# Two row gathers become one over a joined expert table, with pairs handled singly and the top-k made two heads ahead

## The chip, the cores and the metric

The kernel runs on one core of one Trainium2 chip. Times are device microseconds (us) of one execution of the whole program; the time before is a median of three runs. The profile is one further execution, recorded by the hardware profiler. Engines are called as in the profile: PE (TensorE, with PEld for its weight loads), DVE (VectorE), ACT (ScalarE), POOL (GpSimd) and SP (SyncE).

## The reference

Two transformer blocks run one after the other on 512 tokens of width 1024, in float32. The first (neighbourhood attention, a convolution branch, a mixture of experts) and the attention of the second are not touched by the change. What is touched is the last layer, `peer_layer`, for 512 tokens, 8 heads and 16 experts per head:

```python
query = (ht @ w_query).reshape(t, PEER_HEADS, 2, PEER_HALF)
sub_scores = jnp.einsum('thpd,hpkd->thpk', query, sub_keys)          # 2 x 128 scores per head
half_vals, half_idx = lax.top_k(sub_scores, PEER_TOPK)               # 16 of each half
cand = half_vals[:, :, 0, :, None] + half_vals[:, :, 1, None, :]     # 256 sums
top_vals, top_pos = lax.top_k(cand.reshape(...), PEER_TOPK)          # 16 of them
experts = i1 * PEER_N_KEYS + i2                                      # one of 16384 per pick
gates = jax.nn.softmax(top_vals, axis=-1)
...
u = expert_down[eb]                                                  # a row of 1024 per pick
act = jax.nn.gelu(jnp.einsum('td,thkd->thk', xb, u)) * gb
vv = expert_up[eb]                                                   # another row of 1024
return jnp.einsum('thk,thkd->td', act, vv)
```

So each token reads, for each of 8 heads, 16 rows of `expert_down` and the 16 rows of `expert_up` with the same numbers.

## The kernel before

Tokens lie on the 128 partitions, so there are four token tiles t, and a "head" n runs from 0 to 31 (8 heads for each of 4 tiles; `TT = 4`, `H = 8`, `K16 = 16`). All work is ordered by hand: each engine has its own program, and semaphores join them.

**One head.** ACT copies the head's queries to `qh` (`queries`, L1252). PE multiplies them with the sub keys into bank 0 (`peer_scores`, L2371). DVE does the top-k: L1742 to L1746 find 16 of 128 twice, L1759 makes 256 sums, L1742 to L1746 find 16 of these, L1766 prepares the softmax, L1768 to L1777 work out the expert numbers, and L1780 writes them to `ids`. ACT does the softmax's exponential (`gate_exp`, L1256). POOL gathers rows of 4 KB for each of 128 partitions: L837 from the down table and L847 from the up table, 16 of each per head, one indirect DMA for each pick. DVE makes the dot products (L1794), four picks to a group; ACT applies Gelu to four (L1260); DVE multiplies by the gates (`gated`, L1800); ACT makes a diagonal matrix for each pick (L1267); PE multiplies this with the up row, in two halves of 512 columns, and sums over all heads in PSUM (`up_sums`, L2380).

**Buffers.** There are 8 buffers for down rows (two sets of four) and 8 for up rows while tile 0 is worked on, 16 after that. A set of four comes free at once: the down set after its fourth dot product (`down_free`), the up set after its last product on PE (`up_free`).

**Order.** In `gathers`, POOL first waits for the head's `ids`, then issues group by group (down 0, down 1, up 0, down 2, up 1, down 3, up 2, up 3). On DVE the whole top-k of head n+1 stands between dot groups 1 and 2 of head n:

```python
dot(n, t, 0)
dot(n, t, 1)
gated(n, b, 0)
if more:
    topk_halves(nxt)
    topk_pairs(nxt, 1 - b)
    gates(nxt, 1 - b)
dot(n, t, 2)
```

**Tile 0.** Its 8 heads run together with the attention of the tiles 1 to 3 of the same block. That attention is cut into steps (`attend`), and `PLAN` spreads the steps 6 to 66 over 8 heads of 8 parts each, by weights; the two last are projections of the queries for head 0 and 1 of the later tiles (`query_b`, L1875). The other six `query_b` run on PE during the heads of tile 1; SP loads 1 MB of weights for each.

**End of a tile.** `last_norm` on DVE and ACT adds the tile's sums to the residual, normalises and lets SP write it out. PE closes a tile's sums with L2404.

Of the kernel before, what the change touches and what calls it, by code (L numbers as in the profile page):

```python
# [25 lines left out]
P = 128  # L26
T = 512
# [28 lines left out]
G4 = 4  # L56
DOWN_SETS = 2
GROUPS = K16 // G4
UP_FIRST, UP_SETS = 2, GROUPS

# [17 lines left out]
def build(nc, A, out):  # L78
    with ExitStack() as ctx:
# [196 lines left out]
        gate_p = [small(704 + K16 * i, K16) for i in range(2)]  # L276
# [10 lines left out]
        up += [hold_b[:, 3 * D:4 * D], arena_q[:, 3 * D:4 * D], arena_h[:, 0:D], arena_h[:, D:2 * D]]  # L287
        up += [hold_a[:, 2 * D:3 * D], hold_a[:, 3 * D:4 * D], arena_v[:, 6144:6144 + D], arena_v[:, 7168:7168 + D]]

        def up_set(n, g):  # L290

            per = 16 * G4
            if n[1] < H:
                return g % UP_FIRST, (per * GROUPS // UP_FIRST, per * (g // UP_FIRST + 1))
            at = (g + UP_FIRST) % GROUPS
            before = per * GROUPS // UP_FIRST * H if at < UP_FIRST else 0
            return at, (per, per + before - per * H)


        def up_used(n, g):  # L300

            return at_head(n, GROUPS, UP_FIRST + g + 1)
# [11 lines left out]
        x_in = sem("x_in")  # L314
        modb_in = sem("modb_in")
        cw_in = sem("cw_in")
        modb2_in = sem("modb2_in")
        modb3_in = sem("modb3_in")
        rpb_in = sem("rpb_in")
# [5 lines left out]
        mcol2_in = sem("mcol2_in")  # L325
        mod_out_rest = sem("mod_out_rest")
        mcol_in = sem("mcol_in")
        xres_in = sem("xres_in")
# [62 lines left out]
        fn_in = sem("fn_in")  # L391
# [47 lines left out]
        down_free = sem("down_free")  # L439
        up_free = sem("up_free")  # L440
# [7 lines left out]
        last_rows_in = sem("last_rows_in")  # L448
        down_in = [sem(f"down_in{i}") for i in range(DOWN_SETS)]
        up_in = [sem(f"up_in{i}") for i in range(UP_SETS)]  # L450
# [102 lines left out]
        EXP_LN = "natural_log_exp_and_others"  # L553

# [19 lines left out]
        AHEAD = 2  # L574
        STEPS = ST_QUERY + AHEAD
# [4 lines left out]
        PLAN = [[[s for s in range(LEAD, STEPS) if int(sum(weight[LEAD:s]) / sum(weight[LEAD:]) * (H * PARTS - 4)) == h * PARTS + p]  # L580
# [5 lines left out]

        def at_head(n, per, extra):

            i, off = n
            return per * off + extra if i is None else i * (2 * per) + (per * off + extra)  # L590
# [15 lines left out]
        def _(sp):  # L606
# [110 lines left out]
            for dst, src in ((gt2_2, mod2_d[0, 5 * D:6 * D]), (gfin, A["g_final_2"])):  # L717
                sp.dma_start(dst, src.partition_broadcast(P)).then_inc(last_rows_in, 16)
# [5 lines left out]
            sp.wait_ge(skew_out, 16)  # L724
# [4 lines left out]
        def _(pool):  # L729
# [21 lines left out]
            for r, dst in ((0, mcol), (1, mcol_c)):  # L751
# [5 lines left out]
                           A["rpb"].rearrange("h r c -> (h r) c")).then_inc(rpb_in, 16)  # L757
            pool.wait_ge(rpb_in, 16)
# [17 lines left out]
            pool.wait_ge(skew_out, 16)  # L776
# [23 lines left out]
            pool.dma_start(mcol_2[:, :, :], mod2_d[0, 0:2 * D].rearrange("(k p c) -> p k c", k=2, c=DC)).then_inc(mcol2_in, 16)  # L800
# [9 lines left out]
            pool.dma_start(fn_b, A["final_norm"].partition_broadcast(P)).then_inc(fn_in, 16)  # L810
# [19 lines left out]
            pool.sem_inc(down_free, DOWN_SETS)  # L830

            def down_rows(n, b, g):
                pool.wait_ge(down_free, at_head(n, GROUPS, g + 1))
                pool.sem_inc(mark, 1)
                for k in range(G4):
                    r = G4 * g + k
                    pool.indirect_dma_start(down[r % (G4 * DOWN_SETS)], None, A["expert_down_2"],  # L837
                                            bass.IndirectOffsetOnAxis(ap=ids[b][:, r:r + 1], axis=0)).then_inc(down_in[g % DOWN_SETS], 16)

            def up_rows(n, b, g):  # L840
                at, _ = up_set(n, g)

                pool.wait_ge(up_free, up_used(n, g - (UP_FIRST if n[1] < H else UP_SETS)))
                pool.sem_inc(mark, 1)
                for k in range(G4):
                    r = G4 * g + k
                    pool.indirect_dma_start(up[G4 * at + k], None, A["expert_up_2"],  # L847
                                            bass.IndirectOffsetOnAxis(ap=ids[b][:, r:r + 1], axis=0)).then_inc(up_in[at], 16)

            def ids_ready(n):  # L850
                pool.wait_ge(ids_done, at_head(n, 1, 1))
                pool.sem_inc(mark, 1)

            def gathers(n, b):
                ids_ready(n)
                down_rows(n, b, 0)
                for g in range(1, GROUPS):
                    down_rows(n, b, g)
                    up_rows(n, b, g - 1)
                up_rows(n, b, GROUPS - 1)  # L860


            ids_ready((None, 0))
            down_rows((None, 0), 0, 0)
            down_rows((None, 0), 0, 1)
            for h in range(H):
                n, nxt, b = (None, h), (None, h + 1), h % 2
                for g in range(2):
                    down_rows(n, b, 2 + g)
                    up_rows(n, b, g)  # L870
                if h + 1 < H:
                    ids_ready(nxt)
                for g in range(2):
                    if h + 1 < H:
                        down_rows(nxt, 1 - b, g)
                    up_rows(n, b, 2 + g)

            pool.wait_ge(qh_done, H + 1)
            pool.wait_ge(q_done, 4 + 2 * AHEAD)
            for t in range(1, TT):  # L880
                with pool.Fori(0, H // 2) as i:
                    for b in range(2):
                        gathers((i, t * H + b), b)

        @block.scalar
        def _(act):
# [48 lines left out]
            for m in range(18):  # L935
# [12 lines left out]
                if m == 9:  # L948

                    for i, b in enumerate((A["b_mod"][4 * T:8 * T], A["b_mod"][8 * T:12 * T], A["b_ada_2"][0:4 * T])):  # L950
                        act.dma_start(mod_bias[i][0:P:32, :], b.rearrange("(j n) -> j n", n=T)).then_inc(modb2_in, 16)
# [291 lines left out]
            def queries(n):  # L1243
                i, off = n
                if off > 0:
                    act.wait_ge(sc_pe, at_head(n, 1, 0))
                    act.sem_inc(mark, 1)
                if i is None:
                    src = qT2_a[:, off, :] if off < H else qT2_b[:, off - H, :]
                else:  # L1250
                    src = qT2_b[:, bass.ds(i * 2 + (off - H), 1), :].rearrange("p a b -> p (a b)")
                act.activation(qh.rearrange("p a b -> p (a b)"), src, ACT.Copy).then_inc(qh_done, 1)  # L1252
# [17 lines left out]
            def peer_head(n, more, query=None):  # L1270
# [3 lines left out]
                if more:  # L1274
                    queries(nxt)
# [1193 lines left out]
```

## Time and profile before

| | |
|---|---|
| median of 3 runs | 3359.75 us (3359.63 to 3369.18) |
| span of the profiled execution | 3579.5 us |
| PE busy | 2668.3 us, 75% of the span |
| DVE busy | 1426.3 us, 40% |
| POOL busy | 1154.3 us, 32% |
| ACT busy | 709.3 us, 20% |
| DMA, mean over the span | 259 GB/s |
| mean granted TensorE clock | 0.856 |

The profiled execution is 219.75 us longer than the median, 6.5%. Its own time is therefore its span, first to last instruction; nothing of it lies outside. Times from the profile are compared with this span, and carried over to the median by the ratio 3359.75 / 3579.5 = 0.939. Busy shares are means over stages with different limits, so they are read stage by stage below.

### The profile page before, as it was taken

How to read it: one execution, taken by the hardware profiler on the slowest of the kernel's cores; microseconds unless marked ns; L12 is line 12 of the kernel's file. 1: busy time of each engine (PE TensorE's matmuls, PEld its weight loads, DVE VectorE, ACT ScalarE, POOL GpSimd, SP SyncE). 2: the span in 40 equal slices, each digit the busy share in tenths (PEclk: the TensorE clock that was granted, in tenths of full speed). 3: DMA queues.
4: the chain of work that ended last, by engine and by line, in shares of the span. 5: the costliest groups of instructions: out<-in, count | busy, mean ns of one | idle time of the engine just before them, and what ended most of it. 6: DMA issues, size and time to landing. Idle time of an engine off the chain costs nothing.

```text
span 3579.5 us, 28389 instructions
## 1 busy us (share of the span) xinstructions
PE 2668.3 (75%) x8698; PEld 1311.5 (37%) x8698; DVE 1426.3 (40%) x3490; ACT 709.3 (20%) x1634; POOL 1154.3 (32%) x1113
## 2 busy tenths in 40 slices
PE   2998999767777766988779987767675565475566
PEld 1445544423333323556555434333332222232232
DVE  1376400410000003014655465544555555555554
ACT  2015400110000003122342322111112121121111
POOL 1001100000000000001434454656565666666665
PEclk8999999778889987988888899888887787787788
DMA  7328618369999964212666677888887888888887
GB/s 248 128 71 292 210 51 241 143 263 384 377 382 389 397 259 164 94 47 89 239 233 245 248 276 258 315 319 298 307 321 295 335 313 312 313 318 307 320 297 277
DMA packets 281055, 927.91 MB, mean 259 GB/s; under 512 B 27001, under 2 KB 67000, under 8 KB 264062
## 3 DMA queue, kind: packets, MB, share of 16 engines
q0 software_dynamic: 154432, 558.29, 42.6%
q1 hardware_dynamic: 116736, 359.68, 27.4%
q10 hardware_dynamic: 9790, 8.73, 0.7%
q8 instruction: 51, 0.84, 0.1%
q14 instruction: 46, 0.38, 0.0%
HBM read 891.42 MB, written 35.18 MB: 259 GB/s over the span
## 4 chain that ended last, share of the span: by engine, by line
PE 43%; DVE 13%; issue 10%; DVEq 4%; ACT 3%; DMA 2%; POOL 2%; ACTq 1%; another core or an unknown queue 1%; POOLq 0%; SPq 0%
PE bank L2380 18%; PE bank L2081 8%; PE bank L1875 6%; DVE ring L1794 4%; PE bank L2094 3%; DVEq L1737 3%; PE bank L1881 2%; DVEq L1739 1%; POOL ring L837 1%; DMA ring<-in_expert_down,ids 1%; ACTq L1049 1%; ACT arena_h L1267 1%; DVE arena_w L1776 1%; PE bank L2204 1%
## 5 line engine op out<-in xcount | busy, mean ns | idle before, releaser
L2380 PE MATMUL bank<-ring,arena_h 128*128 128x512 f32 x1568 | 771.2, 648 | 508.2 <-ACT arena_h L1267 484.0
L837 POOL DMA_INDIRECT ring<-in_expert_down,ids x512 | 559.0, 1092 | 929.2 <-DVE ids L1780 474.3
L2380 PEld LDWEIGHTS bank<-ring,arena_h 128*128 128x128 f32 x1568 | 321.6, 210 | 916.8 <-ACT arena_h L1267 503.6
L1794 DVE CUSTOM_DVE_ANT_0 ring<-ring 128x1024 f32<-128x1024 f32 x384 | 447.8, 1223 | 204.9 <-DMA ring<-in_expert_down,ids 162.1
L847 POOL DMA_INDIRECT ring<-in_expert_up,ids x392 | 392.3, 1001 | 141.6 <-issue 118.2
L1875 PE MATMUL bank<-arena_h,ring 128*128 128x512 f32 (+1 forms) x1024 | 372.1, 524 | 17.6 <-DMA ring<-in_w_in 15.4
L2081 PE MATMUL bank<-ring,arena_h 128*64 128x512 f32 x1056 | 289.7, 710 | 65.0 <-ACT arena_h L1040 61.9
L1875 PEld LDWEIGHTS bank<-arena_h,ring 128*128 128x128 f32 x1024 | 178.5, 196 | 200.4 <-issue 197.4
L1576 DVE TENSOR_TENSOR arena_q<-arena_q,bank 128x256 f32<-128x256 f32 x32 | 13.5, 421 | 525.2 <-ACT arena_q L1043 525.2
L824 POOL DMA_INDIRECT arena_v<-ys_d,slot_i x8 | 8.0, 1001 | 601.6 <-SPq L675 591.4
L2081 PEld LDWEIGHTS bank<-ring,arena_h 128*64 128x64 f32 x1056 | 98.8, 161 | 231.4 <-issue 196.3
L1794 DVE CUSTOM_DVE_ANT_0 ring<-ring,arena_w 128x1024 f32<-128x1024 f32 x128 | 149.3, 1222 | 56.0 <-DMA ring<-in_expert_down,ids 44.3
L1267 ACT ACTIVATE arena_h<-ident,arena_w 128x128 f32<-128x128 f32 x512 | 159.0, 388 | 6.6 <-DVE arena_w L1800 6.0
L1260 ACT ACTIVATE arena_w<-arena_w 128x4 f32<-128x4 f32 x128 | 24.3, 202 | 626.2 <-DVE arena_w L1794 605.4
L2094 PE MATMUL bank<-ring,arena_q 128*64 128x512 f32 x528 | 120.6, 597 | 21.1 <-DVE arena_q L1579 20.5
L1881 PE MATMUL bank<-ring,arena_h 128*128 128x512 f32 x224 | 101.2, 612 | 1.0 <-ACT arena_h L1203 0.8
L1417 DVE SCALAR_TENSOR_TENSOR arena_x<-arena_x,convc 128x512 f32<-128x512 f32 x120 | 90.2, 752 | 4.3
L1256 ACT ACTIVATE arena_w<-arena_w 128x16 f32<-128x16 f32 x32 | 6.9, 216 | 401.2 <-DVEq L1771 148.7
L2380 PE MATMUL bank<-arena_v,arena_h 128*128 128x512 f32 x192 | 86.3, 592 | 0.0
L2380 PE MATMUL bank<-arena_h 128*128 128x512 f32 x192 | 86.3, 592 | 0.0
L1875 PE MATMUL bank<-arena_q,ring 128*128 128x384 f32 x224 | 80.0, 514 | 8.1 <-issue 8.1
L768 POOL DMA_DIRECT2D mod_d<-arena_v x20 | 10.0, 500 | 232.3 <-DVE arena_v L1402 230.2
(453 smaller groups left out, 3113.3 us busy)
## 6 DMA issues: line engine op xcount, KB each, us to landing
ring<-in_w_exp_gate SPq DMA_DIRECT2D x33, 2048.0 KB, 7.9
ring<-in_w_exp_up SPq DMA_DIRECT2D x33, 2048.0 KB, 12.7
ring<-in_w_exp_down SPq DMA_DIRECT2D x33, 2048.0 KB, 14.3
ring<-in_w_in SPq DMA_DIRECT2D x15, 2048.0 KB, 23.3
ring<-in_w_mod SPq DMA_DIRECT2D x12, 2048.0 KB, 9.8
ring<-in_w_ada SPq DMA_DIRECT2D x12, 2048.0 KB, 16.9
xs_d<-zeros SPq DMA_DIRECT2D x1, 12032.0 KB, 69.5
arena_h<-xs_d SPq DMA_DIRECT2D x33, 256.0 KB, 13.7
```

The lines of the kernel that those rows point to most:

```text
L837: pool.indirect_dma_start(down[r % (G4 * DOWN_SETS)], None, A["expert_down_2"], bass.IndirectOffsetOnAxis(ap=ids[b][:, r:r + 1], axis=0)). ...
L847: pool.indirect_dma_start(up[G4 * at + k], None, A["expert_up_2"], bass.IndirectOffsetOnAxis(ap=ids[b][:, r:r + 1], axis=0)).then_inc(up_i ...
L1049: act.dma_start(ys_d[bass.ds(e * CAP, CAP), 512 * half:512 * half + 512], yblk[b][CAP * half:CAP * half + CAP, :]).then_inc(y_dma[b], 16)
L1267: d = act.activation(diag[:, r, :], ident[:, :], ACT.Copy, scale=coef[:, r:r + 1])
L1417: link(dve.scalar_tensor_tensor(out=conv[:, cc, :], in0=u_pad[:, cc, k:k + T], scalar=convc[:, cc, k:k + 1], in1=conv[:, cc, :], op0=ALU.m ...
L1737: dve.wait_ge(topk_step, at_head(n, TOPK_STEPS, k))
L1794: d = dve.tensor_tensor_reduce(buf, buf, h2r_2[t], 1.0, 0.0, ALU.mult, ALU.add, dots[:, r:r + 1])
L1875: mm = pe.matmul(dst, w[:, c, at], rhs[:, c, :], start=(c == 0), stop=(c == chunks - 1))
L1881: mm = pe.matmul(dst, xT[:, c, t * P:(t + 1) * P], w[:, c, at], start=(c == 0), stop=(c == chunks - 1))
L2081: mm = pe.matmul(bank[2 + b][at, :].rearrange("p (g f) -> p g f", g=2), xbT[b][:, c, :], gu[:, :, c, 256 * half:256 * half + 256], start=( ...
L2094: mm = pe.matmul(bank[6 + b][CAP * j:CAP * j + CAP, :], hidT[b][:, k, CAP * half:CAP * half + CAP], slab(n)[:, half, k, 512 * j:512 * j + ...
L2380: mm = pe.matmul(bank[4 + 2 * (t % 2) + j][:, :], diag[:, G4 * g + k, :], up[G4 * at + k][:, 512 * j:512 * j + 512], start=False, stop=False)
```

## The change

The host joins `expert_down` and `expert_up` side by side into one table with rows of 2048 numbers. One indirect DMA then brings both rows of a pick, 8 KB for each partition, into one "pair" buffer: the dot product reads its first half, PE its second.

- Buffers: 8 pairs for tile 0, 11 after it. Each pair has its own semaphore for landing, and comes free by itself when PE has done its product.
- Top-k: for head n+2 during head n, cut into six pieces, which stand in parts 2 to 7 between pairs of dot products. Top-k of head 1 runs ahead of head 0.
- The multiplication by the gates goes from DVE (one for four picks) to ACT (one for each pick). Gelu takes four picks at once for tile 0 and two after that.
- Attention steps are spread over 6 heads (47 parts) in place of 8 (60 parts). `query_b` 2 to 7 follow the heads 6 to 11, whole.
- `last_norm` of tile t-1 runs after head 6 of the tile t in place of at its end (tile 3's stays at the end). The loops over heads are written out, and some semaphores are merged.

```diff
+PAIRS_0, PAIRS = 8, 11
...
-        down = [ring[:, 2 + r // 4, D * (r % 4):D * (r % 4) + D] for r in range(G4 * DOWN_SETS)]
-        up = [ring[:, 4 + r // 4, D * (r % 4):D * (r % 4) + D] for r in range(G4 * UP_FIRST)]
...
+        pair = [ring[:, 2 + k // 2, 2 * D * (k % 2):2 * D * (k % 2) + 2 * D] for k in range(PAIRS_0)]
+        pair += [hold_a[:, 2 * D:4 * D], arena_v[:, 6144:6144 + 2 * D], arena_h[:, 0:2 * D]]
...
+        LAST_AT = 6
...
+        FRONT = 6
...
-        PLAN = [[[s for s in range(LEAD, STEPS) if int(sum(weight[LEAD:s]) / sum(weight[LEAD:]) * (H * PARTS - 4)) == h * PARTS + p]
+        PLAN = [[[s for s in range(LEAD, STEPS) if int(sum(weight[LEAD:s]) / sum(weight[LEAD:]) * (FRONT * PARTS - 1)) == h * PARTS + p]
...
+            for n in range(TT * H):
+                pool.wait_ge(ids_done, n + 1)
+                for r in range(K16):
+                    m = n * K16 + r
...
+                    if pair_before(m) >= 0:
+                        pool.wait_ge(pair_free, pair_before(m) + 1)
+                    pool.sem_inc(mark, 1)
+                    pool.indirect_dma_start(pair[pair_of(m)], None, A["expert_pair_2"],
+                                            bass.IndirectOffsetOnAxis(ap=ids[n % 2][:, r:r + 1], axis=0)).then_inc(pair_in[pair_of(m)], 16)
...
+            def coefs(n, r0, count):
+
+                m = n * K16 + r0
+                act.wait_ge(dots_done, m + count)
+                act.activation(gel[:, r0:r0 + count], dots[:, r0:r0 + count], ACT.Gelu).then_inc(gelu_done, 1)
+                act.wait_ge(gelu_done, m // count + 1 + (0 if n < H else FIRST // 4 - FIRST // 2))
+                for r in range(r0, r0 + count):
+                    act.activation(coef[:, r:r + 1], gel[:, r:r + 1], ACT.Copy, scale=gate_p[n % 3][:, r:r + 1]).then_inc(coef_done, 1)
+                act.wait_ge(coef_done, m + count)
+                if n > 0:
+                    act.wait_ge(pair_free, m + count - K16)
+                for r in range(r0, r0 + count):
+                    act.activation(diag[:, r, :], ident[:, :], ACT.Copy, scale=coef[:, r:r + 1]).then_inc(diag_done, 1)
...
+            def topk_part(n, part):
+
+                if part in (2, 3):
+                    topk_half(n, part - 2)
                 elif part == 4:
+                    topk_sums(n)
                 elif part == 5:
+                    topk_pairs(n)
                 elif part == 6:
+                    topk_halves_of(n, 0)
                 elif part == 7:
+                    topk_halves_of(n, 1)
+                    topk_ids(n)
+
+            def dot(n, r):
+                m = n * K16 + r
+                dve.wait_ge(pair_in[pair_of(m)], 16 * pair_turn(m))
+                buf = pair[pair_of(m)][:, 0:D]
+                dve.tensor_tensor_reduce(buf, buf, h2r_2[n // H], 1.0, 0.0, ALU.mult, ALU.add, dots[:, r:r + 1]).then_inc(dots_done, 1)
+
+            def peer_part(n, part):
+                dot(n, 2 * part)
+                dot(n, 2 * part + 1)
+                if n + 2 < TT * H:
+                    topk_part(n + 2, part)
...
+            def up_sums(n, r):
+                m = n * K16 + r
+                pe.wait_ge(diag_done, m + 1)
+                for j in range(2):
+                    mm = pe.matmul(bank[4 + 2 * (n // H % 2) + j][:, :], diag[:, r, :], pair[pair_of(m)][:, D + 512 * j:D + 512 * j + 512],
+                                   start=False, stop=False)
+                mm.then_inc(pair_free, 1)
...
+    inputs["expert_pair_2"] = np.concatenate([inputs["expert_down_2"], inputs["expert_up_2"]], axis=-1)
```

## Rows read from the trace of the kernel before

**Rows 1.** The page: engines, granted clock and DMA by slice of the span.
```profile
span 3579.5 us, 28389 instructions
PE 2668.3 (75%) x8698; PEld 1311.5 (37%) x8698; DVE 1426.3 (40%) x3490; ACT 709.3 (20%) x1634; POOL 1154.3 (32%) x1113
...
PEclk8999999778889987988888899888887787787788
DMA  7328618369999964212666677888887888888887
```

**Rows 2.** Four stages: busy us of each engine, granted clock, DMA share, GB/s.
```profile
1000.00:1300.00 300.00, 238.64 (x1011) 94.64 (x1009) 14.38 (x34) 26.84 (x51) 0.00 (x0) 0.91 1.00 390
1670.00:2244.00 574.00, 491.25 (x1733) 284.77 (x1732) 333.33 (x819) 187.70 (x417) 262.95 (x251) 0.87 0.68 244
2244.00:2642.00 398.00, 281.62 (x667) 131.93 (x665) 195.44 (x512) 66.23 (x182) 245.74 (x229) 0.85 0.86 320
2642.00:3552.00 910.00, 532.01 (x1182) 233.73 (x1183) 510.31 (x1295) 172.06 (x447) 586.53 (x542) 0.79 0.84 313
```

**Rows 3.** Timeline: expert numbers of heads 0, 15, 31 written; PE's L2404, first and last.
```profile
1670.01 0.17 DVE L1780 CAST ids<-arena_w 128x16 int32<-128x16 f32 x1
...
2642.54 0.17 DVE L1780 CAST ids<-arena_w 128x16 int32<-128x16 f32 x1
3497.23 0.17 DVE L1780 CAST ids<-arena_w 128x16 int32<-128x16 f32 x1
...
L2404 PE MATMUL bank<-zeros x32: 592/592/595, 1671.3 to 3568.7; 128*128 128x512 f32 x32
```

**Rows 4.** Timeline of POOL over one head: start, us, instruction, [idle before].
```profile
3023.29 1.21 POOL L837 DMA_INDIRECT ring<-in_expert_down,ids  x1 [9.47 <-DVE arena_w L1794]
3024.81 1.98 POOL L837 DMA_INDIRECT ring<-in_expert_down,ids  x1 [0.30 <-issue]
3027.09 0.94 POOL L837 DMA_INDIRECT ring<-in_expert_down,ids  x1 [0.30 <-issue]
3028.34 0.94 POOL L837 DMA_INDIRECT ring<-in_expert_down,ids  x1 [0.30 <-issue]
...
3066.88 0.93 POOL L847 DMA_INDIRECT ring<-in_expert_up,ids  x1 [0.31 <-issue]
3076.49 1.21 POOL L837 DMA_INDIRECT ring<-in_expert_down,ids  x1 [8.68 <-DVE arena_w L1794]
```

**Rows 5.** Top-k of head 0 on DVE, with POOL idle: first and last but one.
```profile
1657.30 0.30 DVE L1742 MAX8 arena_w<-bank 128x8 f32<-128x128 f32 x1 [20.61 <-PE bank L2371]
...
1669.80 0.17 DVE L1777 SCALAR_TENSOR_TENSOR arena_w<-arena_w 128x16 f32<-128x16 f32 x1
```

**Rows 6.** Dot products and top-k of one later head on DVE, with POOL issuing.
```profile
3034.12 1.23 DVE L1794 CUSTOM_DVE_ANT_0 ring<-ring 128x1024 f32<-128x1024 f32 x1 [6.55 <-DMA ring<-in_expert_down,ids]
3035.27 0.08 DVE L1794 DVE_READ_ACCUMULATOR2_ANT arena_w<- 128x1 f32 x1
3035.27 1.22 DVE L1794 CUSTOM_DVE_ANT_0 ring<-ring 128x1024 f32<-128x1024 f32 x1
...
3046.87 0.30 DVE L1742 MAX8 arena_w<-bank 128x8 f32<-128x128 f32 x1 [2.49 <-PE bank L2371]
...
3059.01 0.43 DVE L1773 TENSOR_TENSOR arena_w<-iota,arena_w 128x256 f32<-128x256 f32 x1 [2.46 <-issue]
...
3068.78 0.17 DVE L1780 CAST ids<-arena_w 128x16 int32<-128x16 f32 x1 [1.93 <-issue]
```

**Rows 7.** Short stretches within one head; columns as in Rows 2.
```profile
3020.00:3025.00 5.00, 1.02 (x2) 0.51 (x3) 5.00 (x12) 1.41 (x5) 1.40 (x2) 0.50 0.00 0
3025.00:3030.00 5.00, 5.00 (x11) 2.28 (x10) 2.38 (x6) 2.81 (x10) 4.08 (x4) 0.81 0.81 243
...
3055.00:3060.00 5.00, 0.00 (x0) 0.00 (x0) 1.60 (x7) 1.59 (x3) 3.78 (x5) 0.76 1.03 419
3060.00:3065.00 5.00, 0.00 (x0) 0.00 (x0) 1.70 (x4) 0.00 (x0) 3.78 (x5) 0.50 1.03 410
```

**Rows 8.** Timeline of PE: products of up rows and a `query_b`.
```profile
2213.12 7.03 PE L2380 MATMUL bank<-ring,arena_h 128*128 128x512 f32 x16
2219.98 10.48 PE L1875 MATMUL bank<-arena_q,arena_v 128*128 128x384 f32 x32
```

**Rows 9.** PE's L2380 alone in the tile 0 stage: busy, clock, DMA share, GB/s.
```profile
1670.00:2244.00 574.00, 228.90 (x475) 0.87 0.68 244
```

**Rows 10.** Groups of instructions on ACT.
```profile
L1267 ACT ACTIVATE arena_h<-ident,arena_w 128x128 f32<-128x128 f32 x512 | 159.0, 388 | 6.6 <-DVE arena_w L1800 6.0 <-issue 0.4
L1260 ACT ACT_TABLE_LOAD x45 | 57.7, 1283 | 0.8
L1260 ACT ACTIVATE arena_w<-arena_w 128x4 f32<-128x4 f32 x128 | 24.3, 202 | 626.2 <-DVE arena_w L1794 605.4 <-issue 20.6
```

More of the change, by code:

```diff
@@ L275, in build @@
         gsub, gex = small(672, K16), small(688, K16)
-        gate_p = [small(704 + K16 * i, K16) for i in range(2)]
+        gate_p = [small(704 + K16 * i, K16) for i in range(2)] + [sb("gate_c", [P, K16])[:, :]]
         dots, gel, coef = small(736, K16), small(752, K16), small(768, K16)
@@ L447, in build @@
         rows2_in = sem("rows2_in")
-        last_rows_in = sem("last_rows_in")
-        down_in = [sem(f"down_in{i}") for i in range(DOWN_SETS)]
-        up_in = [sem(f"up_in{i}") for i in range(UP_SETS)]
+        pair_in = [sem(f"pair_in{i}") for i in range(PAIRS)]
         yg_in = [sem(f"yg_in{t}") for t in range(TT)]
@@ L854, in gathers @@
[L854 to L876, printed above, removed]
@@ new lines, in peer_head @@
+            def peer_head(n):
+                for p in range(PARTS):
+                    if p == 0 and n + 2 < TT * H:
+                        queries(n + 2)
+                    if p == 6 and n + 2 < TT * H:
+                        gate_exp(n + 2)
+                    coefs(n, 2 * p, 2)
+            def peer_part(n, part):
+                if part == 0:
+                    queries(n + 2)
+                if part == 6:
+                    gate_exp(n + 2)
+                if part % 2 == 1:
+                    coefs(n, 2 * part - 2, 4)
+                    if any(s < ST_FOX for parts in PLAN[n:] for steps in parts for s in steps):
+                        act.preload_act_table_set(EXP_LN)
@@ L1789, in dot @@
-            def dot(n, t, g):
-                dve.wait_ge(down_in[g % DOWN_SETS], at_head(n, 16 * G4 * (GROUPS // DOWN_SETS), 16 * G4 * (g // DOWN_SETS + 1)))
-                for k in range(G4):
-                    r = G4 * g + k
-                    buf = down[r % (G4 * DOWN_SETS)]
-                    d = dve.tensor_tensor_reduce(buf, buf, h2r_2[t], 1.0, 0.0, ALU.mult, ALU.add, dots[:, r:r + 1])
-                d.then_inc(down_free, 1)
-            def gated(n, b, g):
-                at = slice(G4 * g, G4 * g + G4)
-                dve.wait_ge(gelu_done, at_head(n, GROUPS, g + 1))
-                dve.tensor_tensor(coef[:, at], gel[:, at], gate_p[b][:, at], ALU.mult).then_inc(coef_done, 1)
@@ L1856, in _ @@
                         attend(s)
[L1857 to L1867 removed]
+            for n in range(H, TT * H):
+                for part in range(PARTS):
+                    peer_part(n, part)
+                if n % H == LAST_AT:
+                    if n // H == 1:
+                        dve.wait_ge(rows2_in, 16 * 10)
+                    last_norm(n // H - 1)
             last_norm(TT - 1)
@@ L2401, in edge, with peer_part @@
+            def peer_part(n, part):
+                if part == 1:
+                    peer_scores(n + 2)
+                if part % 2 == 0 and n + part > 0:
+                    for r in range(4):
+                        up_sums(n if part else n - 1, (2 * part - 4 + r) % K16)
             def edge(t, first):
```

366 lines of the change are left out of this document (116 added, 250 removed).

## The prediction

> **What bounds the kernel now.** I read the page's slices first, then the stages, then one head on POOL, DVE and the DMA engines. On the page [rows 1] no engine but PE is over 40% busy, while in the last two fifths the DMA digit stands at 7 or 8. The stages [rows 2] say where this begins. Tile 0 with attention beside it (1670 to 2244 us) has PE busy for 491 of 574 us and DMA at 0.68. Afterwards PE is busy 58% of the time (532 of 910 us), DVE 56%, POOL 64% and the DMA engines 0.84 at 313 GB/s. So in the later stage no resource is full, and the question is what leaves them idle in turn.
>
> Rows 3 give the pace: from head 15's numbers to head 31's there are 16 heads in 854.7 us, 53.4 us each. One head on POOL [rows 4] shows what fills it. From 3023.29 to 3067.81 POOL issues 32 gathers without a pause; the common one takes 0.94 us and 0.30 us of issue, 1.24 us, and some take 1.98. That is 44.5 us. Then POOL stands for 8.68 us, until DVE has made dot products again. DVE has not made any because the top-k stands between its dot groups: with POOL idle the top-k takes 12.9 us (1657.30 to 1670.18) [rows 3, 5], with POOL issuing it takes 22 us (3046.87 to 3068.95), with waits such as 2.46 us in front of an operation [rows 6]. So the loop is POOL's 32 issues, plus a hole made by the top-k: 44.5 + 8.7 = 53.2 us. In the hole the DMA engines run dry (0.00 and 0 GB/s), while just before they run at 410 to 419 GB/s [rows 7]. PE, which gets its pairs late, stands too, and its granted clock is at 0.50 (1.2 GHz) in the slice before its restart and 0.81 in the slice after.
>
> **The change, part by part.** I cost the stretch from the first head's numbers (1670.2) to the last product (3568.7): 1898.5 us [rows 3]. The 1670 us ahead are left as they are but for merged semaphores, which I cost at nothing, as the same transfers are waited for. The 10 us behind (the last norm) stay.
>
> *Later heads, 12 to 31.* The bytes stay: 16 picks x 128 rows x 8 KB = 16.78 MB a head.
> - POOL: 16 issues in place of 32. If a pair costs what a row does, 16 x 1.24 = 19.8 us, and if each meets a dot product and takes 1.98 + 0.30, 36.5 us. No trace row has a gather of 8 KB rows. Below, I take the same cost, since the number of rows to be addressed is the same; above, twice 0.94. Either way POOL can be under the DMA time.
> - DVE: 16 dots at a pitch of 1.15 us [rows 6] are 18.4 us; a wait ahead of each may add 0.1, so 20. The top-k is 12.9 us with POOL idle and 22 with POOL always issuing. POOL would issue for 1.24 of each 2.7 us, so about half of the 9 us extra: 17.5. `gated` is gone. Sum 37.5 us, under the DMA time but near it.
> - ACT: per two picks one Gelu (0.20), two coefficients (about 0.20 each, as the small Gelu) and two diagonals (0.39 each) [rows 10], 1.4 us, and with the hand-overs some 2 us; 8 x 2 = 16, and two table loads of 1.28: 19 us. The coefficients that moved here (3.2 us a head) are hidden behind a DMA pace of 5.4 us for two picks.
> - PE: 64 records a head at 7.03 / 16 = 0.44 us [rows 8] is 28 us at full clock.
> - DMA: the longest saturated stretch of this trace moved 390 GB/s at share 1.00 for 300 us [rows 2]; the gathers reach 410 to 419 for some 15 us [rows 7]. 16.78 MB take 43.0 us at 390, 40.4 at 415, 45.0 at 373 (313 / 0.84, what a full share would give at this stage's efficiency). I take 43.0, because it is the rate that was held longest.
> - Buffers: a pair lives from issue to PE's product. From the end of the fourth issue (3029.28) to the dot of that group (3034.12) are 4.8 us. Add 1.2 for the issue, up to 3.5 for a piece of top-k in front, 2.4 for two dots, 2 for ACT, 3.5 for two products on PE: 17.4 us. Eleven buffers at 2.7 us cover 29.6 us, so the gathers stay ahead and POOL no longer waits on DVE's top-k. The numbers for head n+1 are there before head n begins, so this wait goes altogether.
> So 20 x 43.0 = 860 us. The stall moves from POOL to the DMA queue.
>
> The Trainium skill, "DMA: Bandwidth & Descriptors", section Specifications, gives a limit of about 358 GB/s of HBM for a core. By that a head would take 46.9 us and this change would give 26 x 3.9 = 101 us less of what I count. The trace has 390 and 419 GB/s, so it disagrees, and the sum goes by its rows.
>
> *Heads 6 to 11.* Each has a `query_b` behind it on PE, 32 records, 10.5 us [rows 8]: 28 + 10.5 is 38.5 us, still under DMA. SP's 1 MB of weights adds 1.05 / 0.39 = 2.7 us of DMA: 45.7. Heads 6 and 7 have 8 buffers and four picks to a Gelu: life of a pair near 24 us over 8 buffers is 3.0 us a pick, 48 us. So 2 x 48 + 4 x 45.7 = 279 us.
>
> *Heads 0 to 5, with the attention.* In 1670 to 2244, PE was busy 491.25 us, of which L2380 had 228.9 [rows 9]; the rest, 262 us, is attention and projections and must now fit in six heads. With six heads of products, 228.9 x 6 / 8 = 172, PE has 434 us. It stood for 83 us over 8 heads, 10.3 a head. Some of that was waiting for down rows behind late numbers, which goes; against this ACT swaps tables four times a head where it did twice, 2 x 2 x 1.28 = 5 us, and each step follows a longer chain. I keep 7.6 a head, 46 us. The early top-k of head 1 (12.9 us) stands where nothing of head 0 can run: 10 us. Sum 490 us. Bounds: 434 (no idle) to 584 (the old 574 us untouched, plus 10).
>
> *Total.* 490 + 279 + 860 = 1629 us for 1898.5: 270 us less, 3579.5 - 270 = 3309.5 us in the profile's own time. The median of the runs is shorter by 6.1%, so times 0.939: 3106 us. I say 3105.
>
> **The rivals.** All are counted in the median's time.
> - *DVE becomes the bound.* POOL's issues and DVE's operations hold each other up [rows 6]: with POOL issuing, the top-k takes 9 us more. If all of that stays and dots wait too, DVE needs 20 + 22 + 6 = 48 us a head. Heads 6 to 31: 1248 for 1139, +102: 3208 us. For it speaks that 37.5 is near 43; against it that POOL is silent half the time.
> - The Trainium skill, "SBUF — State Buffer", section SBUF: two separate sides, says that DVE and GpSimd share a port pair under an exclusive lock that is held for a whole instruction. The row's 2.46 us before L1773 agrees; by it alone half as many issues lock half as long.
> - *The front does not shrink.* If chains across engines, not PE, set tile 0, the steps take what they took: 584 us for 490, +88: 3193 us. For it: PE's 83 us idle. Against: PE busy 86%.
> - *DMA is slower than 390 GB/s.* At 373 the 26 heads take 2 us more each, +49: 3155 us.
> - *An 8 KB gather costs POOL double.* 1.88 + 0.30, and 1.04 more where a dot is met (1.98 - 0.94) [rows 4]: 3.22 x 16 = 51.5 us a head; 24 heads x 8.5 x 0.939, +192: 3300 us.
> - *The recorder slows what the change removes.* The profile is 219.75 us above the median. If all of this lay in POOL's issuing in the 32 heads, a head before takes 46 us unprofiled, and the change gives 270 - 220 = 50 us: 3310 us. Nothing in the trace tells this apart.
> - *Slower: PE stays at 1.2 GHz.* PE would work in bursts of 3.5 us with 1.9 us between them. If the clock stayed at 0.50 (1.2 GHz), the records take twice 0.44: 56 us a head and 77 with a `query_b`, 20 x 56 + 6 x 77 = 1582 for 1139: 3520 us. It decides once PE's own time for a head passes the 53.4 us of before, which needs nearly all of the head at 0.50. For it: PE idles in every head, as it does ahead of the 0.50 in rows 7. Against it: at 0.50 PE would have no idle time left, and in rows 7 the clock is 0.81 as soon as PE is busy through a slice.
> - *Nothing changes*, some loop of the same length taking over: 3360.
>
> **How the numbers follow.** Chances: forecast 0.42 (its own range 3060 to 3160), DVE bound 0.14, front 0.09, slower DMA 0.09, double POOL cost 0.05, recorder 0.09, clock 0.08, nothing 0.04. Faster is all but the last two: 0.88; within 0.3% (about 10 us, what a measurement here can tell from no change) 0.04; slower 0.08. The range begins at 3030: with 40.4 us a head (-63) and a front of 470 (-19) it would be 3024. Upwards it goes to 3310, to the two cases of 3300 and 3310 us, since without them 0.26 would be left out; with them 0.12 is, the two last. It also takes in two of the milder rivals together (3208 and +88).
>
> **What would show it.** Right: from some 2200 us on, the DMA share stays at 1.0 and 390 GB/s or more with no slice near 0; heads 12 to 30 come each 43 us, by the writing of the expert numbers; POOL waits mostly for PE's releases; the granted clock is above 0.9; the sixth head ends some 490 us after the first numbers. Wrong: DVE over 95% busy (DVE bound); gathers of near 1.9 us (double cost); PE busy throughout with the clock at 0.5 (clock); heads at 43 us but a median less than 150 us below the old one (recorder); the heads 0 to 5 over 560 us (front).

## The result: 3269 us for 3361 us, a third of the forecast gain

The changed kernel takes 3268.78 us (median of 4 runs, 3263.08 to 3270.47), the kernel before 3360.53 us. The ratio is 0.9703 with a 95% interval of 0.9677 to 0.9729, so it is 92 us faster. I had forecast 3105 us, 255 us faster; the direction is right and the size is not. The changed kernel's own profile spans 3261.3 us, 8 us from its median.

The page of the changed kernel, to be held against [rows 1]:

```profile
span 3261.3 us, 27350 instructions
...
PE 2663.6 (82%) x8698; PEld 1292.5 (40%) x8698; DVE 1425.1 (44%) x3362; ACT 872.7 (27%) x2245; POOL 661.9 (20%) x601
...
PEclk8999999968888989699789877999999999999998
DMA  7417814728999999512136745689999999999996
GB/s 248 164 52 241 300 61 143 244 95 321 386 377 380 393 387 384 199 65 67 38 128 226 290 163 224 243 317 369 418 417 421 421 421 421 421 398 421 421 421 278
```

POOL's busy time fell from 1154 to 662 us, the DMA digit stays at 9 in the last quarter but for the last slice, and the rate there is 421 GB/s in most slices. That is what the prediction described. The next view says what it was worth. These are the stages of the changed kernel by token tile (columns as in [rows 2]); each ends where PE closes the tile's sums:

```profile
1670.00:2267.00 597.00, 530.65 (x1833) 303.79 (x1831) 346.27 (x835) 247.19 (x587) 137.33 (x135) 0.87 0.66 253
2267.00:2599.00 332.00, 284.27 (x681) 126.86 (x680) 237.56 (x583) 118.07 (x364) 152.64 (x131) 0.97 1.01 419
2599.00:2924.00 325.00, 248.91 (x552) 101.58 (x551) 240.42 (x586) 117.39 (x365) 163.16 (x129) 0.97 1.00 415
2924.00:3249.00 325.00, 247.38 (x548) 100.23 (x547) 218.71 (x505) 110.71 (x354) 152.21 (x119) 0.97 0.96 400
```

A later head takes 325 / 8 = 40.6 us (40.7 by the writing of the expert numbers), with a DMA share of 1.00 and a granted clock of 0.97. The stretch I had costed at 1629 us measures 1579 us. So the changed kernel is, if anything, a little better than I had worked out, and the gain is still a third. The error has to be in what it was compared with, and the first experiment asks that.

### The profile page after: what moved, and what is told of

It is laid out like the page before. It is cut to its first block, busy times and chain, and to the rows that moved or that the text cites. A ratio compares the mean times of both kernels' runs of the same rounds, so it can differ in the third digit from the quotient of the medians.

```text
span 3261.3 us, 27350 instructions
## 1 busy us (share of the span) xinstructions
PE 2663.6 (82%) x8698; PEld 1292.5 (40%) x8698; DVE 1425.1 (44%) x3362; ACT 872.7 (27%) x2245; POOL 661.9 (20%) x601
## 4 chain that ended last, share of the span: by engine, by line
PE 38%; DMA 20%; DVE 7%; ACT 6%; issue 4%; ACTq 1%; POOL 1%; DVEq 0%; POOLq 0%; SPq 0%
DMA ring<-in_expert_pair,ids 15%; PE bank L2290 9%; PE bank L1995 9%; PE bank L1789 6%; PE bank L2008 4%; PE bank L1795 3%; DMA arena_v<-in_expert_pair,ids 3%; DVE ring L1744 2%; DMA arena_h<-in_expert_pair,ids 1%; ACTq L1002 1%; PE bank L2118 1%; PE bank L2117 1%; ACT arena_h L1219 1%; POOL ring L835 1%; ACT arena_w L1214 1%
## 5 line engine op out<-in xcount | busy, mean ns | idle before, releaser
L2290 PE MATMUL bank<-ring,arena_h 128*128 128x512 f32 x1772 | 840.9, 624 | 183.0 <-ACT arena_h L1219 182.9
L835 POOL DMA_INDIRECT ring<-in_expert_pair,ids x443 | 519.5, 1173 | 1161.3 <-PE bank L2290 633.0
L2290 PEld LDWEIGHTS bank<-ring,arena_h 128*128 128x128 f32 x1772 | 340.0, 198 | 652.6 <-issue 370.2
L1744 DVE CUSTOM_DVE_ANT_0 ring<-ring 128x1024 f32<-128x1024 f32 x315 | 383.8, 1225 | 177.3 <-DMA ring<-in_expert_pair,ids 158.0
L1789 PE MATMUL bank<-arena_h,ring 128*128 128x512 f32 (+1 forms) x1024 | 373.0, 525 | 15.6 <-DMA ring<-in_w_in 13.5
L1211 ACT ACTIVATE arena_w<-arena_w 128x2 f32<-128x2 f32 (+1 forms) x224 | 45.4, 203 | 627.1 <-DVE arena_w L1744 626.8
L1219 ACT ACTIVATE arena_h<-ident,arena_w 128x128 f32<-128x128 f32 x512 | 174.1, 393 | 7.3
L1795 PE MATMUL bank<-ring,arena_h 128*128 128x512 f32 x224 | 100.9, 610 | 1.0 <-ACT arena_h L1156 0.8
L2290 PE MATMUL bank<-arena_v,arena_h 128*128 128x512 f32 x140 | 70.3, 626 | 21.5 <-ACT arena_h L1219 21.5
L1214 ACT ACTIVATE arena_w<-arena_w 128x1 f32<-128x1 f32 x352 | 81.8, 285 | 5.0
L1795 PE MATMUL bank<-ring,arena_q 128*128 128x512 f32 x176 | 78.9, 609 | 3.6 <-DVE arena_q L1406 3.6
L2290 PE MATMUL bank<-arena_h 128*128 128x512 f32 x136 | 66.8, 614 | 17.5 <-ACT arena_h L1219 17.5
```

The source lines that it names most:

```text
L835: pool.indirect_dma_start(pair[pair_of(m)], None, A["expert_pair_2"], bass.IndirectOffsetOnAxis(ap=ids[n % 2][:, r:r + 1], axis=0)).then_i ...
L1211: act.activation(gel[:, r0:r0 + count], dots[:, r0:r0 + count], ACT.Gelu).then_inc(gelu_done, 1)
L1214: act.activation(coef[:, r:r + 1], gel[:, r:r + 1], ACT.Copy, scale=gate_p[n % 3][:, r:r + 1]).then_inc(coef_done, 1)
L1219: act.activation(diag[:, r, :], ident[:, :], ACT.Copy, scale=coef[:, r:r + 1]).then_inc(diag_done, 1)
L1744: dve.tensor_tensor_reduce(buf, buf, h2r_2[n // H], 1.0, 0.0, ALU.mult, ALU.add, dots[:, r:r + 1]).then_inc(dots_done, 1)
L1789: mm = pe.matmul(dst, w[:, c, at], rhs[:, c, :], start=(c == 0), stop=(c == chunks - 1))
```

## The experiments

### The kernel before, recorded once more

The file is unchanged.

> The kernel before, unchanged, once more. Theory A (the profiled execution on which the prediction stood was itself about 220 us slower than the median runs, in the gather stage, and the changed kernel's own profile is not): this execution has a span within 10 us of 3360, its stretch up to 1670 us is as before, and heads 15 to 31 come every 46 us or so in place of 53.4. Rival B (recording always adds 220 us to the kernel before): the span is again near 3580 and only the unrecorded runs are near 3360. Ratio to the kernel before 1.00 either way.

Measured: ratio 1.0003 (0.9977 to 1.003), and a profile that spans 3374.5 us, not 3579.5. Theory A holds, though the span is 14.5 us above 3360 where I had said within 10, and the first numbers come at 1678 us, 8 us later. The same four tiles in this second recording:

```profile
1676.00:2254.00 578.00, 513.76 (x1789) 293.93 (x1789) 340.77 (x833) 191.72 (x428) 282.80 (x268) 0.87 0.70 257
2254.00:2637.00 383.00, 312.74 (x745) 146.31 (x744) 243.15 (x622) 80.63 (x218) 282.15 (x260) 0.90 0.98 372
2637.00:2996.00 359.00, 255.69 (x553) 111.77 (x552) 237.95 (x616) 83.75 (x211) 281.83 (x254) 0.86 0.98 370
2996.00:3363.00 367.00, 265.03 (x551) 114.54 (x550) 225.78 (x573) 75.05 (x202) 279.26 (x245) 0.85 0.95 356
```

A head of tiles 2 and 3 takes 45.4 us (726 / 16), not the 53.4 us of [rows 3]. The hole that the prediction made its first term is not there. Its POOL timeline shows a stretch with dot products, then the top-k (2908.9 to 2921.8), then dot products again:

```profile
2901.45 1.98 POOL L847 DMA_INDIRECT arena_h<-in_expert_up,ids  x1 [0.30 <-issue]
2903.74 0.93 POOL L847 DMA_INDIRECT arena_h<-in_expert_up,ids  x1 [0.30 <-issue]
2904.98 1.27 POOL L837 DMA_INDIRECT ring<-in_expert_down,ids  x1 [0.30 <-issue]
2906.56 1.98 POOL L837 DMA_INDIRECT ring<-in_expert_down,ids  x1 [0.31 <-issue]
2908.84 0.94 POOL L837 DMA_INDIRECT ring<-in_expert_down,ids  x1 [0.30 <-issue]
...
2917.54 0.94 POOL L837 DMA_INDIRECT ring<-in_expert_down,ids  x1 [0.31 <-issue]
...
2922.79 1.59 POOL L847 DMA_INDIRECT ring<-in_expert_up,ids  x1 [0.31 <-issue]
2924.69 1.98 POOL L847 DMA_INDIRECT ring<-in_expert_up,ids  x1 [0.30 <-issue]
```

POOL never waits for anyone; it only issues. And the top-k takes 13 us with POOL issuing beside it, as it does with POOL idle [rows 5], against 22 us in [rows 6]. From 2650 to 3050 us the 281 gathers take 1.123 us in the mean, and with 0.30 us of issue 32 of them are 45.5 us: the pace of a head. Among the 281, 41 take 1.7 us or more and 18 between 1.1 and 1.7; most of the rest are at 0.94.

The long issues are those that meet a dot product. These are the dot products during which the issues at 2904.98 and 2922.79 began, and a like pair of rows of the changed kernel, with 8 KB rows:

```profile
2904.21 1.23 DVE L1794 CUSTOM_DVE_ANT_0 ring<-ring 128x1024 f32<-128x1024 f32 x1 [0.43 <-DMA ring<-in_expert_down,ids]
2922.35 1.23 DVE L1794 CUSTOM_DVE_ANT_0 ring<-ring 128x1024 f32<-128x1024 f32 x1 [0.16 <-DVE arena_w L1786]
```
```profile
2800.39 1.23 DVE L1744 CUSTOM_DVE_ANT_0 ring<-ring 128x1024 f32<-128x1024 f32 x1 [0.43 <-DMA ring<-in_expert_pair,ids]
2800.67 1.75 POOL L835 DMA_INDIRECT ring<-in_expert_pair,ids  x1 [1.98 <-PE bank L2290]
```

The issues begin 0.77, 0.44 and 0.28 us after their dot product and take 1.27, 1.59 and 1.75 us: each ends 2.03 to 2.04 us after the dot product began. From 2650 to 3050 us this is so for every issue that begins 0.06 to 1.08 us after a dot product, 24 of 24 here and 75 of 75 in the changed kernel. So the issue stands until some 1.09 us of the dot product are over and then takes its own 0.94. One that begins within 0.05 us of the start mostly takes 1.98 and sometimes 0.94.

That leaves two readings. Either POOL's issuing is the bound, with its long issues, or the DMA engines are (their share is 0.98) and the long issues are a symptom of that.

### Two gathers for each pair

```diff
-                    pool.indirect_dma_start(pair[pair_of(m)], None, A["expert_pair_2"],
+                    for j, table in enumerate(("expert_down_2", "expert_up_2")):
+                        pool.indirect_dma_start(pair[pair_of(m)][:, j * D:(j + 1) * D], None, A[table],
```

> The changed kernel, but each pair is brought by two gathers of 4 KB rows from the two separate tables into the two halves of the pair buffer; all else stays. Theory A (the gain is that the gathers run ahead without a hole and the DMA engines stay full; the joined table only saves issues): POOL has 32 issues of 1.24 us a head, 39.7 us and up to 50 where dot products hold them up, so POOL, not DMA, sets the heads 15 to 31: 45 to 50 us in place of 40.8, total 3350 to 3400. Rival B (POOL's issues still hide under the DMA time): 41 to 43 us a head, total 3270 to 3310.

Measured: 3358.69 us, ratio 0.9985 (0.996 to 1.001). A head takes 44.5 and 45.4 us in tiles 2 and 3 (356.0 and 363.4 us). All the rest of the change (pairs handled singly, the top-k two heads ahead in pieces, gates on ACT) brings nothing in sum by itself; joining the gathers on top of it brings the whole gain. The sum hides two parts: against the second recording of the kernel before, tile 0 is 27 us longer here, tile 1 35 us shorter (two of its six `query_b`, 21 us of PE, now lie in tile 0) and tiles 2 and 3 3 us shorter each. Joining then takes 5, 17, 30 and 39 us off the four tiles. Joining the gathers without the rest was not tried. And 45 us a head fits both readings still, POOL's issuing and full DMA engines.

### Half of the bytes, with the same issues

```diff
+                        w = D if n < H else D // 2
+                        at = j * D + (w * (pair_turn(m) % 2) if n >= H else 0)
+                        pool.indirect_dma_start(pair[pair_of(m)][:, at:at + w], None,
+                                                A[table] if n < H else A[table].rearrange("e (a b) -> (e a) b", b=w),
```

> As the kernel with two gathers a pair, but from head 8 on each gather brings only 512 of the 1024 columns of a row (2 KB a partition), and the other half of the buffer keeps older rows; dot products and products on PE stay as long. So 32 issues a head as before, with half of the bytes. Theory A (with 4 KB rows POOL's issuing sets the pace: 32 x 1.24 us plus some 5.5 long ones x 1.04, 45.4 us a head): tiles 2 and 3 stay near 356 and 363 us, total 3340 to 3370, and the DMA share falls to some 0.55. Rival B (the DMA engines are full at 370 to 375 GB/s with 4 KB rows, their share being 0.98 to 0.99): the pace falls to the next limit, 38 to 41 us a head, total near 3230 to 3270.

Measured: 3415.66 us, ratio 1.0106 (1.0066 to 1.0146). With half of the bytes no head is faster; in tiles 2 and 3 they take 47.7 and 47.0 us, for 44.5 and 45.4. That is above the range of theory A (3340 to 3370 us) and far from rival B. The windows 2650 to 3050 us, first the two gathers of 4 KB rows, then of 2 KB:

```profile
2650.00:3050.00 400.00, 291.76 (x616) 118.23 (x617) 270.30 (x658) 131.77 (x410) 312.77 (x287) 0.94 0.99 378
```
```profile
2650.00:3050.00 400.00, 282.16 (x578) 113.36 (x577) 253.58 (x621) 121.72 (x380) 318.43 (x268) 0.92 0.62 177
```

The kernel before, in its second recording, has in the same window:

```profile
2650.00:3050.00 400.00, 283.17 (x606) 123.87 (x607) 264.88 (x676) 92.78 (x237) 314.59 (x281) 0.85 0.98 369
```

So the DMA engines were not the bound at 378 GB/s with two gathers a pair, although their share read 0.99. POOL is busy 313 to 318 of 400 us in all three, which with 0.30 us for each issue leaves it no idle time. The 2 KB kernel even has more long issues (56 of 268, for 29 of 287), and (1.189 + 0.30) us x 32 = 47.6 us is again its pace. That is why it is slower and not only no faster; why more of its issues meet a dot product was not looked into.

### Short dot products

The dot products take 256 of the 1024 columns and leave the others out; bytes and issues stay. The edit was made in three kernels: with two gathers a pair, for the kernel before, and for the changed kernel.

```diff
-                dve.tensor_tensor_reduce(buf, buf, h2r_2[n // H], 1.0, ...
+                buf = pair[pair_of(m)][:, 0:D // 4]
+                dve.tensor_tensor_reduce(buf, buf, h2r_2[n // H][:, 0:D // 4], 1.0, ...
```

> As the kernel with two gathers a pair, but the dot products read and write only 256 of the 1024 columns (some 0.4 us in place of 1.22). Bytes and issues stay. Theory A (POOL sets the pace and its long issues of 1.98 us are those that meet a dot product): the long issues nearly go, 39.7 to 41 us a head, total 3359 - 24 x 4.5 = about 3250, at 410 GB/s. Rival B (DMA full at 375 GB/s with 4 KB rows, long issues being a full ring): 45 us a head as before, total 3340 to 3360.

> The kernel before, but the dot products read and write only 256 of the 1024 columns, as in the short-dot kernel with two gathers a pair. Theory A (in the kernel before, too, POOL's 32 issues and those of them that a dot product holds up set the pace, 32 x 1.24 + 5.5 x 1.04 = 45.4 us a head): 40 to 42 us a head, total 3366 - 24 x 4 to 5 = 3245 to 3275, ratio 0.965 to 0.973. Rival B (in the kernel before the top-k or DVE's dots are on the path as the prediction said): the gain comes from DVE, 24 x 16 x 0.8 = 307 us less, ratio 0.91.

> The changed kernel, but the dot products read and write only 256 of the 1024 columns. Theory A (its heads 12 to 31 wait for the DMA engines at 421 GB/s, and POOL has time to spare): the later tiles stay within 2 us of 325, total 3250 to 3270 with a little less in tile 0. Rival B (POOL or DVE is close under the DMA time and takes part): total under 3240.

Measured: two gathers a pair 3278.57 us, ratio 0.9699 (0.9661 to 0.9738); the kernel before 3248.05 us, 0.9636 (0.9615 to 0.9658); the changed kernel 3248.38 us, 0.9651 (0.9623 to 0.9679). The groups on POOL from 2650 to 3050 us (instructions, busy us, mean ns, idle before and its releasers), first of the kernel before, second recording, then of the same with short dots:

```profile
L837 POOL DMA_INDIRECT ring<-in_expert_down,ids x140 | 145.1, 1036 | 42.7 <-issue 42.1 <-PE bank L2380 0.6
L847 POOL DMA_INDIRECT ring<-in_expert_up,ids x98 | 118.5, 1209 | 29.9 <-issue 29.0 <-DVE ids L1780 0.9
```
```profile
L837 POOL DMA_INDIRECT ring<-in_expert_down,ids x154 | 146.4, 951 | 57.2 <-issue 43.9 <-DVE arena_w L1794 13.3
L847 POOL DMA_INDIRECT ring<-in_expert_up,ids x106 | 101.9, 961 | 32.3 <-issue 29.3 <-DVE ids L1780 2.7 <-DVE arena_w L1794 0.3
```

Of 310 issues none takes 1.7 us; the head takes 41.4 us in tiles 2 and 3, and the rate is 409 GB/s. With two gathers a pair the head falls to 41.8 and 41.6 us, a little above the 39.7 to 41 expected, also at 409 GB/s. Nothing on the DMA side was changed. So the issues held up by dot products are what held the kernel before. The rival for the kernel before, DVE itself on the path, wanted a ratio of 0.91 and is out.

With the long issues gone, the kernel before and the changed kernel take the same time within their spread, 3248.05 and 3248.38 us. That equality is a sum of unequal parts: the tiles are 552, 350, 331 and 331 us in the one, 581, 330, 325 and 324 in the other. The later tiles of the changed kernel stay at 325.1 and 324.4 us with short dots: there POOL had time to spare. With full dot products it already waits, mostly until PE frees a pair:

```profile
L835 POOL DMA_INDIRECT ring<-in_expert_pair,ids x131 | 167.5, 1278 | 155.7 <-PE bank L2290 131.3 <-issue 24.4
```

The two next experiments tell whether the DMA engines or the number of buffers set that wait. The changed kernel's 20 us come from tiles 0 and 1, which were 596 and 332 us and are 581 and 330; I had expected 0 to 19.

### What would be next under the DMA time

One gather of 4 KB a pair in place of 8 (half of the bytes; PE multiplies what the buffer held before):

```diff
-                    pool.indirect_dma_start(pair[pair_of(m)], None, A["expert_pair_2"],
+                    pool.indirect_dma_start(pair[pair_of(m)][:, 0:D], None,
+                                            A["expert_pair_2"].rearrange("e (a b) -> (e a) b", b=D),
```

> The changed kernel, but each gather brings 4 KB a partition instead of 8 (one row of 1024 numbers of the joined table viewed as rows of 1024), into the first half of the pair buffer; PE multiplies what was there. 16 issues a head and half of the bytes. Theory A (the heads 12 to 31 are set by the DMA engines at 421 GB/s, 40.7 us): the pace falls to DVE's or ACT's own time, 34 to 39 us a head, total 3269 - 24 x 2 to 6 = 3130 to 3220. Rival B (something else is at 40.7 us too): total within 15 us of 3269. Tile 0, which PE and the attention set, stays at 590 to 600 us.

Measured: 3083.87 us, ratio 0.9124 (0.9088 to 0.916). Tile 0 is 576 us, tiles 1 to 3 are 297, 263 and 253 us.

```profile
2650.00:3050.00 400.00, 363.57 (x837) 154.34 (x836) 355.56 (x866) 181.08 (x567) 237.25 (x198) 0.98 0.78 261
```

With half of the bytes the changed kernel does get faster, by 8 to 9 us a head, where the one with 32 issues did not: in its later heads the transfers are the bound. At 31.6 to 32.8 us PE (364 of 400 us) and DVE (356) are nearly full; which of them is next was not tried. Two of my figures were off. I had 34 to 39 us a head and 3130 to 3220 us in all, because DVE's 37.5 us was too high: its operations are hardly held up. And I had tile 0 unchanged at 590 to 600 us, but it too is 20 us shorter.

### The buffers and the pieces

```diff
-PAIRS_0, PAIRS = 8, 11
+PAIRS_0, PAIRS = 8, 8
```

> The changed kernel with 8 pair buffers throughout in place of 11. Theory A (a pair lives some 17 us, so 8 buffers at 2.55 us a pick, 20.4 us, still suffice): heads 15 to 31 stay within 42 us, total within 25 us of 3269. Rival B (a pair lives 25 us or more, and the eleven buffers are what makes the DMA engines full): 50 us a head, total 3269 + 17 x 9 = about 3420.

Measured: 3281.89 us, ratio 0.9751 (0.9695 to 0.9807). Tiles 2 and 3 take 326 and 325 us, as with eleven; tile 1, which in this kernel has four of the six later `query_b`, takes 346 us for 332. Eight buffers carry the steady pace, so the number of buffers does not set it. The three buffers more bring their time in tile 1; the likely reason, not tried by itself, is that the `query_b` blocks hold PE for 10.5 us at a time there.

The pieces of the top-k as one block at the end of each later head:

```diff
+                    elif part == PARTS - 1:
+                        for piece in range(PARTS):
+                            topk_part(n + 2, piece)
```

> The changed kernel, but from head 8 on the six pieces of the top-k stand as one block of 13 us at the end of the head, behind its last dot product, and the softmax's exponential behind ACT's last picks. Theory A (11 pairs at 2.55 us are 28 us of transfers, and a pair lives 17 us, so a hole of 13 us on DVE is just about covered): tiles 1 to 3 grow by 0 to 2 us a head, total 3265 to 3315. Rival B (cutting the top-k is needed to keep the DMA engines full): the hole reaches them, 4 us a head or more, total above 3360, which would give the whole gain back.

Measured: 3286.68 us, ratio 0.9753 (0.9725 to 0.9781). Tiles 1 and 2 take 342 and 331 us for 332 and 325, tile 3 323. So a hole of 13 us on DVE costs at most 1.3 us a head, and cutting the top-k is worth some 20 us of the gain, not all of it.

### A better split of the attention

In heads 6 and 7 of the changed kernel PE has no attention steps and waits for pairs. This version spreads the steps over 53 parts in place of 47. The top-k of head 8 must then come a head later, so from head 7 on it is one head ahead, in parts 0 to 5 (the edits on ACT and PE that follow from it are left out here):

```diff
-        FRONT = 6
+        FRONT = 7
...
-(FRONT * PARTS - 1)) == h * PARTS + p]
+(FRONT * PARTS - 3)) == h * PARTS + p]
...
-                if n + 2 < TT * H:
+                if n < 6:
                     topk_part(n + 2, part)
+                elif n >= 7 and n + 1 < TT * H:
+                    topk_part(n + 1, part + 2)
```

> The changed kernel with its attention steps spread over 53 parts (6.6 heads) in place of 47, which needs the top-k of head 8 a head later: heads 0 to 5 make the top-k two ahead as they do, head 6 makes none, and from head 7 on it is one ahead, its six pieces in parts 0 to 5 so that the numbers are there four picks before the head ends. Theory A (tile 0 is set by PE and its chain with the attention; in heads 6 and 7 PE stands 30 to 40 us of 111, which attention can fill): tile 0 falls from 596 to 570 to 585 us, later tiles stay within 3 us, total 3245 to 3262. Rival B (the top-k one ahead leaves the gathers short of numbers, 2 us or more a head): the later tiles grow by 16 us each, total 3290 or more.

Measured: 3259.06 us, ratio 0.9641 (0.961 to 0.9672); tile 0 576 us, tile 1 336 us, the others 326. The edit also shifts the `query_b` by one head, so that tile 0 has one of them where it had two (2235 us, for 2202 and 2249 us) and tile 1 five: 10.5 us of PE leave tile 0 together with the better spread. Both kernels were then run side by side:

> The changed kernel, unchanged, on the same chip as the two others of this call, so that they can be compared with it directly. Expected: ratio to the kernel before 0.970 within 0.005, tile 0 near 596 us, tiles 2 and 3 near 325 us.

> The kernel with attention steps over 53 parts, once more, beside the changed kernel on the same chip. Theory A (its 20 us shorter tile 0, 576 us for 596, is real and tile 1 gives back 4): ratio to the kernel before 0.005 below that of the changed kernel, that is near 0.965. Rival B (the shorter time came from the chip of that call): both within 0.002 of each other.

Measured: the changed kernel 3267.3 us, 0.9702 (0.9679 to 0.9725); this one 3251.68 us, 0.9657 (0.9632 to 0.9681). Tile 0 is 20 us shorter in both of its recordings and tile 1 4 us longer. The medians are 15.6 us apart, 0.5%. The two intervals against the kernel before just touch, so the size is less sure than the direction. How much of the 20 us is the spread of the attention and how much the moved `query_b` is not told apart.

## Why the prediction was wrong

- **The comparison, which failed.** "From head 15's numbers to head 31's there are 16 heads in 854.7 us, 53.4 us each" was true of that one execution. In the second recording the same heads take 45.4 us. The step "so times 0.939" spread the 219.75 us between profile and median over the whole span, but nearly all of them lay in the later heads: the four tiles of the first profile take 595, 461, 427 and 413 us by PE's L2404, of the second 574, 383, 359 and 367. The three later ones differ by 192 us. I had the warning (a rival gave it 0.09) and put its cause in recording as such. The runs show otherwise: the second recording of the same kernel is within 8 us of its median. In the second recording the stretch that I costed is 1686 us long; against it the same sum of 1629 us would have given 57 us less, some 3300 us.
- **The hole.** "So the loop is POOL's 32 issues, plus a hole made by the top-k: 44.5 + 8.7" names a second term that the second recording does not have. The first term is the whole loop, 45.4 to 45.5 us.
- **The sum for the changed kernel held.** Front 490 us: the first six heads' numbers span 474. Heads 6 to 11 279 us: 286. Heads 12 to 31 860 us: some 817. The terms were off by 16, 7 and 43 us, the last because of the DMA rate: I took 390 GB/s, and the gathers of 8 KB rows hold 421, 40.7 us a head for 43.
- **POOL.** A gather of 8 KB rows costs what one of 4 KB does, 938 ns in the median, so my lower bound was right; 1.27 us in the mean with those held up. Of "if each meets a dot product and takes 1.98" some 40% do (60 of 159 take 1.7 us or more, most of them 1.75).
- **The path of the gain.** I said it would be the hole. It is the long issues: 32 x 0.94 + 32 x 0.30 = 39.7 us would have been under the DMA time; some five long ones and two half-long ones a head put it at 45.5. Halving the issues takes POOL off the path and leaves 40.7 us of DMA. The clean measure of this is the kernel with two gathers a pair: 3358.69 - 3268.78 = 90 us. Between the kernel before and the changed one, the later three tiles give 1109 - 982 = 127 us and tile 0 takes back 22 (596 for 574). The moved `query_b` 2 and 3 (21 us of PE) would be enough for that and for as much of tile 1's gain, but no run moves them alone.
- **The rivals.** Neither DVE nor the clock became a bound (granted clock 0.97, DVE 240 of 325 us). HBM did not stop at 358 GB/s: the Trainium skill ("DMA: Bandwidth & Descriptors", section Specifications) has that limit, and 400 to 419 GB/s over whole tiles, 421 in single slices, are above it. The Trainium skill ("HBM Reference", section Specifications (TRN2)) makes that a share for two cores that stream together and gives about 425 GB/s for a core alone; with that the trace agrees. The front did not stay at its old length.

What stays open is why the first recorded execution was 205 us longer than the second. Where the time lies can be said: in tiles 1 to 3 a top-k, from its first L1742 to L1780, takes 22.4 us in the median of the first recording and 13.0 in that of the second, 9.4 us more where a head is 8.0 us longer. The instructions are as long; DVE stands between them. Before L1773 alone it stood for 40 us in 28 places, with nothing to wait for that the profile shows; in the second it did not do so at all. The views of that line in the first and the second recording:

```profile
L1773 DVE TENSOR_TENSOR arena_w<-iota,arena_w x64: 424/425/487, 1667.1 to 3493.8; 128x256 f32<-128x256 f32 x64
...
  issue: 40.0, 28
```
```profile
L1773 DVE TENSOR_TENSOR arena_w<-iota,arena_w x64: 424/425/427, 1675.0 to 3289.7; 128x256 f32<-128x256 f32 x64
```

The slowest of all the timed runs of the kernel before took 3399.36 us, so it was not seen again, and no experiment on it was tried.

## What to carry to other kernels

When a profile's span and the median of the runs differ by as much as the gain at stake, the profile shows another execution than the one that is timed: record the kernel again before its stalls are priced, and carry a difference over stage by stage, not by a ratio. An indirect gather of 128 rows cost its issuing engine the same for rows of 2, 4 and 8 KB, so joining tables that are read with the same indices halves that cost; here it paid as far as issuing, held up by the dot products on DVE, was longer than the transfers. A DMA share near 1 does not show that the DMA engines are the bound; halve the bytes or the hold-ups and look at the pace.

## What the runs showed of the hardware

- DMA engines read as full while they could move more: share 0.98 at 369 GB/s, where the same engines moved 409 GB/s of the same 4 KB rows at share 1.03 once POOL was not held up.
- A gather's issue that begins during a dot product of 1.22 us stands until that is nearly over and then takes its 0.94 us, up to 1.98 us in all; with dots of 256 columns none of 310 is above 1.7 us. The dot products themselves keep their 1.15 us pitch. The Trainium skill ("SBUF — State Buffer", section SBUF: two separate sides) has an exclusive lock between DVE and GpSimd that is held for a whole instruction; the 24 of 24 and 75 of 75 issues that end 2.03 to 2.04 us after their dot product began agree. In the second recording POOL waits and DVE does not, so the 2.46 us before L1773 that I had counted for the lock are not there. In the first the top-k on DVE was 9.4 us longer a head; whether that is DVE waiting for POOL is not shown.
- Rows of 8 KB moved at 421 GB/s. Rows of 4 KB with short dots moved at 409 GB/s, but there POOL was taken for some 390 of 400 us (310 issues of 0.954 + 0.30 us), so it is not shown that the 3% are those of the row's length.
- A gather's issue took 0.94 us in the median with rows of 8, 4 and 2 KB, and the next began 0.30 us later at the soonest.
